# A first mixer's beginning reordered: the condition matvec in four column groups, weight chunks woven between it, late modulation rows moved

## The chip, the cores and the metric

The kernel runs on one core of a Trainium2 chip. The metric is the device time of one execution in microseconds, the median of several. The profile is of one execution; its span is counted from the first to the last instruction. The core has five instruction streams: TensorE (PE, matmuls into PSUM), VectorE (DVE), ScalarE (ACT), GpSimd (POOL) and SyncE (SP, here it issues the DMAs of the weights). They run side by side and wait for each other by semaphores only.

## The reference

Two transformer blocks on 512 tokens of 1024 features, all in fp32. Only the beginning of the first one matters here:

```python
mod_x = (jax.nn.silu(c) @ w_mod[l] + b_mod[l])[:, None, :]
mod_c = jax.nn.silu(c_ctx) @ w_mod[l] + b_mod[l]
sh1, sc1, gt1, sh2, sc2, gt2 = jnp.split(mod_x, N_MOD, axis=-1)
csh1, csc1, cgt1, csh2, csc2, cgt2 = jnp.split(mod_c, N_MOD, axis=-1)
h_x = _modulate(x, g_pre_mix[l], sh1, sc1)       # rmsnorm(x) * (1 + scale) + shift
h_c = _modulate(ctx, g_pre_mix[l], csh1, csc1)
u_x, q_x, k_x, v_x = _project(h_x, w_in[l])      # 1024 x 2048: u, q, k, v of 512 each
u_c, q_c, k_c, v_c = _project(h_c, w_in[l])
attn_x = _neighbourhood_attention(q_x, k_x, v_x, k_c, v_c, rpb[l])
mix_x = jnp.concatenate([_pool_mixer(u_x, pool_w[l], pool_scale[l]), attn_x], axis=-1) @ w_out[l]
```

`w_mod` is 1024 x 6144. Its first two sections (shift and scale, 2048 columns) are needed, for `c` and for `c_ctx`, before any product with `w_in`. The other four are needed for `c` alone, and only later.

## The kernel before

**The stream of weights.** All weights are cut into blocks of 128x128; eight blocks are a chunk of 512 KB. `plan_weights` writes their order down, and SyncE loads the chunks in exactly this order into four buffers `raw`. A chunk is loaded when the user of the chunk four places ahead has let go of its buffer; as SyncE works in order, one late chunk holds up all behind it.

**Splitting.** A product is made of three passes with operands in two parts: a high part rounded to fp32r and the low rest. `ahead` on ScalarE makes the high part `wH` of a chunk (line 1083), `ahead` on GpSimd the low part `wL` (line 2252). There are three buffers of each. The call `ahead(name, k, m)` splits up to three chunks on from the named block, but only such as stand less than four places of the plan behind it (`reach`). The buffer `raw` is free when `wL` is made. Lines 513 to 515 and 550 to 552 are the three passes. The modulation's chunks are not split: those of the first two sections go through TensorE as fp32 matmuls (`first_rows`, line 593), the 32 later ones ("late rows") through VectorE, one multiply-add of 128x1024 each into `macc` (`late_rows`, lines 1667 and 1670). At the end of a section TensorE sums `macc` over the partitions (`late_columns`, line 612).

**The matvec.** The plan begins with 16 chunks `w_mod`, chunk k of a half holding rows 128k of both sections. `first_rows(n)` multiplies the two columns silu(c), silu(c_ctx) with the 1024 columns of the chunk: two matmuls of 512 columns into two banks of two partitions. VectorE copies the two rows out (`first_vectors`, line 1700), `first_columns` (line 602) turns them into columns with eight small matmuls, `first_coefficients` forms shift and scale. The order on TensorE is: chunks 0 to 9, columns of half 0, statistic of x (line 562), chunks 10 to 15. The squares of x are added up by GpSimd (line 2262).

**The norms.** VectorE scales x by the root (line 1732); ScalarE forms `hH` (line 1148), VectorE the full value and every even `hL`, GpSimd every odd `hL` (line 2257). The same is done for ctx: `context_norm` on VectorE (lines 1769, 1775, 1655), `hcH` on ScalarE (line 1181), odd `hcL` on GpSimd.

**The products.** Tiles m=0..3 of `w_in` are u, 4..7 q, 8..11 k, 12..15 v. TensorE works on tiles 0 to 3 as a group (k outside, so that it can start with the first feature block), the statistic of ctx, then tile by tile 4 to 11, tiles 8 to 11 also for ctx and with one pool matmul each (line 659), then the values with tokens as rows (lines 550 to 552). One late row stands in the plan ahead of each of the tiles 4 to 7, two ahead of each of 8 to 11, two behind each value chunk but four more at the end, which VectorE takes up during the attention (one at every eighth step). Behind the values comes the attention: 32 steps of scores (line 569), turn (line 577) and values (line 584), VectorE adding the bias (line 1809), taking the maximum (line 1682) and normalizing (line 1690). The biases `bms` are made by GpSimd (line 2304) from `bra`, which SyncE loads (line 2515).

**One pair of the context norm** stands between two tiles on every engine: ScalarE copies the tile before, then forms two `hcH`; GpSimd splits the tile's chunk, then makes one `hcL`; VectorE does a late row, a pool window and the pair.

## Time and profile before

| | before |
|---|---|
| median of three runs | 1520.77 us (1517.61 to 1526.13) |
| the profiled execution | 1509.5 us, its span 1508.2 us |
| TensorE busy | 1420.2 us, 94% |
| GpSimd / VectorE / ScalarE busy | 48% / 39% / 37% |
| mean granted clock of TensorE | 0.979 |
| first product with `w_in` | 44.06 us |
| last value product, begin of the attention | 182.7 us |
| begin of the product with `w_out` | 281.0 us |

The share of TensorE is an average. A matmul is pipelined, so the duration of one is longer than the distance to the next. In a row of the timeline, the bracket tells how long the engine was idle before the instruction, and which engine's instruction ended that.

### The profile page before, as it was taken

The numbers are of one execution on the slowest core, as the hardware profiler recorded it, in microseconds if no ns is written. First come the engines' busy times: TensorE is split into PE (matmuls) and PEld (weight loads), VectorE is DVE, ScalarE is ACT, GpSimd is POOL, SyncE is SP. The second block draws the span as 40 slices with busy tenths as digits, with TensorE's granted clock in tenths as the row PEclk, the third lists the DMA queues.
The fourth block names the chain that finished last, engine by engine and source line by source line (L and its number), as shares of the span: only waits on it lengthen the run. The fifth ranks groups of instructions, "written<-read, shape, count | busy, mean of one in ns | idle before, by whom it ended". The sixth has DMA issues, their size and how long they took to land.

```text
span 1508.2 us, 16271 instructions
## 1 busy us (share of the span) xinstructions
PE 1420.2 (94%) x6446; PEld 1115.6 (74%) x6446; DVE 589.2 (39%) x872; ACT 551.2 (37%) x865; POOL 717.3 (48%) x387
## 2 busy tenths in 40 slices
PE   8869999988899999999789999999999999999999
PEld 1658766776788887888577778766577788888887
DVE  2592377238342205210362956674444211012110
ACT  3422155354343324422343453653433322122221
POOL 2442343264444443455446957262336655455552
PEclk9989999999999999999899999999999999999999
DMA  8526520323232532333223111111113233233332
GB/s 291 208 103 217 191 81 24 112 82 100 70 112 98 186 115 78 103 98 98 84 56 98 56 43 56 56 57 45 40 43 98 84 98 100 97 97 98 98 98 70
DMA packets 41035, 148.59 MB, mean 99 GB/s; under 512 B 4608, under 2 KB 4864, under 8 KB 40192
## 3 DMA queue, kind: packets, MB, share of 16 engines
q1 hardware_dynamic: 39504, 139.02, 28.7%
q0 software_dynamic: 592, 4.72, 0.9%
q10 hardware_dynamic: 864, 3.82, 0.7%
q8 instruction: 51, 0.84, 0.2%
q14 instruction: 24, 0.20, 0.0%
HBM read 144.65 MB, written 2.10 MB: 97 GB/s over the span
## 4 chain that ended last, share of the span: by engine, by line
PE 73%; DVE 10%; POOL 6%; ACT 5%; issue 4%; DMA 1%; SPq 0%; DVEq 0%; ACTq 0%; POOLq 0%
PE bank L513 20%; PE bank L515 19%; PE bank L514 19%; PE bank L569 3%; POOL wL L2252 3%; PE bank L584 3%; PE bank L562 2%; POOL EE L2399 2%; PE bank L577 1%; DMA raw<-in_wall 1%; PE bank L550 1%; PE bank L552 1%; PE bank L551 1%; DVE xT L1849 1%; ACT wH L1083 1%
## 5 line engine op out<-in xcount | busy, mean ns | idle before, releaser
L2252 POOL TENSOR_TENSOR wL<-raw,wH 128x1024 fp32r<-128x1024 f32 (+1 forms) x205 | 499.4, 2439 | 474.7 <-ACT wH L1083 474.7
L513 PE MATMUL bank<-hH,wH 128*128 128x512 f32 x784 | 320.6, 409 | 41.6 <-POOL wL L2252 26.7
L514 PE MATMUL bank<-hL,wH 128*128 128x512 f32 x784 | 311.1, 397 | 0.0
L515 PE MATMUL bank<-hH,wL 128*128 128x512 f32 x784 | 311.1, 397 | 0.0
L1083 ACT ACTIVATE wH<-raw 128x1024 fp32r<-128x1024 f32 (+1 forms) x205 | 214.6, 1048 | 241.3 <-PE bank L515 168.3
L513 PEld LDWEIGHTS bank<-hH,wH 128*128 128x128 f32 x784 | 151.1, 193 | 82.6 <-issue 43.9
L515 PEld LDWEIGHTS bank<-hH,wL 128*128 128x128 f32 x784 | 150.5, 192 | 33.0
L514 PEld LDWEIGHTS bank<-hL,wH 128*128 128x128 f32 x784 | 151.1, 193 | 30.5 <-issue 1.7
L513 PE MATMUL bank<-gH,wH 128*128 128x512 f32 x352 | 138.2, 393 | 4.1 <-POOL wL L2252 4.1
L514 PE MATMUL bank<-gL,wH 128*128 128x512 f32 x352 | 137.7, 391 | 0.0
L515 PE MATMUL bank<-gH,wL 128*128 128x512 f32 x352 | 137.7, 391 | 0.0
L513 PE MATMUL bank<-bH,wH 128*128 128x512 f32 x256 | 100.4, 392 | 0.0
L515 PE MATMUL bank<-bH,wL 128*128 128x512 f32 x256 | 99.7, 389 | 0.0
L514 PE MATMUL bank<-bL,wH 128*128 128x512 f32 x256 | 99.6, 389 | 0.0
L513 PEld LDWEIGHTS bank<-gH,wH 128*128 128x128 f32 x352 | 66.5, 189 | 19.6 <-issue 5.8
L1113 ACT ACTIVATE P<-bank,small 128x512 f32<-128x512 f32 (+3 forms) x64 | 37.9, 592 | 109.7 <-DVE small L1682 43.0
L515 PEld LDWEIGHTS bank<-gH,wL 128*128 128x128 f32 x352 | 66.5, 189 | 14.0
L514 PEld LDWEIGHTS bank<-gL,wH 128*128 128x128 f32 x352 | 66.4, 189 | 13.9 <-issue 0.2
L2262 POOL TENSOR_TENSOR acc<-acc,tmp 128x512 f32<-128x512 f32 x31 | 41.1, 1326 | 70.6 <-ACT tmp L1107 70.0
L1902 DVE TENSOR_TENSOR tmp<-tmp 128x512 f32<-128x512 f32 x32 | 36.9, 1153 | 90.5 <-ACT tmp L1297 90.5
L1670 DVE SCALAR_TENSOR_TENSOR macc<-raw,vecs,macc 128x1024 f32<-128x1024 f32 x28 | 44.0, 1572 | 38.5 <-DMA raw<-in_wall 37.6
L515 PEld LDWEIGHTS bank<-bH,wL 128*128 128x128 f32 x256 | 48.0, 188 | 10.1
(328 smaller groups left out, 2127.8 us busy)
## 6 DMA issues: line engine op xcount, KB each, us to landing
raw<-in_wall SPq DMA_DIRECT2D x253, 512.0 KB, 3.6
bra<-in_rpbw SPq DMA_DIRECT2D x8, 360.0 KB, 3.3
xq<-in_xt ACTq DMA_DIRECT2D x2, 1024.0 KB, 9.5
xT<-in_xn POOLq DMA_DIRECT2D x1, 2048.0 KB, 8.0
out_x<-xT SPq DMA_DIRECT2D x8, 256.0 KB, 2.0
vE<-in_ctxt ACTq DMA_DIRECT2D x1, 1024.0 KB, 7.9
icn<-in_invc POOLq DMA_DIRECT2D x1, 1024.0 KB, 4.9
xm<-in_memt POOLq DMA_DIRECT2D x1, 1024.0 KB, 6.8
```

The costliest lines, as they stand in the source:

```text
L513: matmul(o, a_h, b_h, start=first, stop=False)
L514: matmul(o, a_h, b_l, start=False, stop=False)
L515: return matmul(o, a_l, b_h, start=False, stop=last)
L562: mm = matmul(o[:, 0:n], ones[lo:hi, :], sq, start=i == 0, stop=i == len(parts) - 1)
L569: mm = matmul(o[:, c0:c1], lhsT, rhs, start=first, stop=last)
L584: mm = matmul(o, v, a.PT[i % 2][:, 128 * n:128 * n + 128], start=n == 0, stop=n == len(values) - 1)
L1083: activation(wH[i % NHL][:, 0:n], raw[c % NRAW][:, 0:n], ACT.Copy).then_inc(s.w_hi, 1)
L1113: activation(a.P[i % 3][:, 0:w], bank[a.sc(i)][:, 0:w], ACT.Exp, bias=small[i % 6][:, 0:1], scale=a.scale, accum_out=small[i % 6][:, 1:2]) ...
L1670: stt(out=macc[:, :], in0=raw[c % NRAW][:, :], scalar=ck, in1=macc[:, :], op0=ALU.mult, op1=ALU.add).then_inc(s.mod_acc, 1)
L1902: tt(t, t, t, ALU.mult).then_inc(s.relu_sq, 1)
L2252: tt(wL[i % NHL][:, 0:n], raw[c % NRAW][:, 0:n], wH[i % NHL][:, 0:n].bitcast(F32), ALU.subtract).then_inc(s.w_lo, 1)
L2262: tt(sums, sums, tm[2 + j % 2][:, :], ALU.add).then_inc(s.add_g, 1)
```

## The change

It moves work within the beginning of the first mixer; the products and sums that are formed are the same.

1. The matvec goes to four column groups. `cond` holds, for each k, silu(c) and silu(c_ctx) in 32 columns, 30 of them zero. The output of matmul i of chunk k goes to the partitions 32(2i + k%2) of bank 6, so that two chunks use four groups; the even and the odd k are summed afterwards. `sel`, a 128x4 matrix of zeros and ones, does that within `first_columns`, which now has four matmuls instead of eight. One copy of 128x512 takes the place of two of 2x512.
2. The plan: 8 matvec chunks, 3 chunks of `w_in` (tiles 0 to 5, k=0..3), 8 matvec chunks, 3 chunks of `w_in` (k=4..7). The first group has six tiles. TensorE takes matvec chunks 8 to 11 behind k=0 and 12 to 15 behind k=1, the second columns behind k=2, the statistic of ctx behind k=7.
3. The squares of x are summed in two halves by GpSimd and VectorE, and the statistic of x is formed between matvec chunks 5 and 6.
4. The pairs of the context norm stand together: all four ahead of tile 6 on VectorE, ScalarE and GpSimd, the splits of tiles 6 and 7 behind them on the latter two, and the copies of u and q behind those.
5. Late rows: none ahead of tile 8, 2, 4, 4 and 6 behind tiles 8 to 11, two behind each value chunk; none is left for the attention. The late columns of sections 2, 3 and 4 stand ahead of tile 11, behind k=1 of the values, and at step 4 of the attention. SyncE's loads of the later biases are moved accordingly.

```diff
@@ -71,16 +71,14 @@
     for half in range(2):
         for k in range(8):
             plan.extend(("w_mod", k, 8 * sec + 4 * half + j, True) for sec in range(2) for j in range(4))
-    group([("w_in", m) for m in range(4)], range(8))
-    for m in range(4, 12):
-        for _ in range(1 if m < 8 else 2):
+        group([("w_in", m) for m in range(6)], range(4 * half, 4 * half + 4))
+    for m in range(6, 12):
+        tile("w_in", m, range(8))
+        for _ in range((0, 0, 2, 4, 4, 6)[m - 6]):
             mod_rows()
-        tile("w_in", m, range(8))
     for k in range(0, 8, 2):
         wide("w_in", 12, range(k, k + 2))
         mod_rows()
-        mod_rows()
-    for _ in range(4):
         mod_rows()
     group([("w_out", m) for m in range(4)], range(8))
     for m in range(4, 8):
@@ -585,22 +586,25 @@
...
         def first_rows(n):
             half, k = divmod(n, 8)
-            pe.wait_ge(raw_in[n % NRAW], 16 * (n // NRAW + 1))
-            pe.wait_ge(s.silu_c, 1)
+            c = ROWS[n]
+            pe.wait_ge(raw_in[c % NRAW], 16 * (c // NRAW + 1))
+            pe.wait_ge(s.silu_c, 2)
+            pe.wait_ge(s.mod_row, half)
             for i in range(2):
-                mm = matmul(bank[2 * half + i][0:2, :], cc[:, 2 * k:2 * k + 2], raw[n % NRAW][:, 512 * i:512 * i + 512],
-                            start=k == 0, stop=k == 7)
+                g = 32 * (2 * i + k % 2)
+                mm = matmul(bank[6][g:g + 32, :], cond[:, k, :], raw[c % NRAW][:, 512 * i:512 * i + 512], start=k < 2,
+                            stop=k >= 6)
             mm.then_inc(s.mod_mm, 1)
         def first_columns(half):
             o = claim(7)
-            pe.wait_ge(s.ident_in, 16)
-            pe.wait_ge(s.mod_row, 2 * half + 2)
-            for j in range(8):
-                mm = matmul(o[:, 2 * j:2 * j + 2], mrow[half][:, 128 * j:128 * j + 128], ident[0:2, 0:2],
-                            start=True, stop=True)
+            pe.wait_ge(s.sel, 3)
+            pe.wait_ge(s.mod_row, half + 1)
+            for j in range(4):
+                mm = matmul(o[:, 4 * j:4 * j + 4], mrow[half][:, 128 * j:128 * j + 128], sel[:, :], start=True, stop=True)
             mm.then_inc(s.mod_col, 1)
             freed[7] = s.mod_ab, 2 * half + 2
@@ -613,16 +617,16 @@
             mm.then_inc(s.mod_sum, 1)
             freed[7] = s.mod_late, sec - 1
-        pe.wait_ge(s.ones, 2)
-        for n in range(10):
+        pe.wait_ge(s.ones, 3)
+        for n in range(6):
             first_rows(n)
-        freed[0:2] = [(s.mod_row, 1), (s.mod_row, 2)]
+        pe.wait_ge(s.add_g, ADD_G.x + 3)
+        pe.wait_ge(s.add_v, ADD_V.x + 3)
+        statistic("x", [(acc[0][:, :], 0, 128), (acc[1][:, :], 0, 128)])
+        first_rows(6)
+        first_rows(7)
         first_columns(0)
-        pe.wait_ge(s.add_g, ADD_G.x + 7)
-        statistic("x", [(acc[0][:, :], 0, 128)])
-        for n in range(10, 16):
-            first_rows(n)
-        freed[2:4] = [(s.mod_row, 3), (s.mod_row, 4)]
+        freed[6] = s.mod_row, 2
         def X1(k):
@@ -631,22 +635,26 @@
         def XC(k):
             return hcH[:, k, :], hcL[:, k, :], s.rest_g if k % 2 else s.rest_v, REST.hc + k // 2 + 1
-        def second_columns(k):
-            if k == 1:
+        def second_half(k):
+            if k < 2:
+                for n in range(8 + 4 * k, 12 + 4 * k):
+                    first_rows(n)
+            if k == 2:
                 first_columns(1)
-        us = [("w_in", m) for m in range(4)]
-        outs = [claim(BANK[t]) for t in us]
-        group(us, range(8), X1, outs, second_columns)
+            if k == 7:
+                pe.wait_ge(s.add_v, ADD_V.c + 7)
+                statistic("ctx", [(acc[1][:, 0:256], 0, 128)], 256)
+        first = [("w_in", m) for m in range(6)]
+        group(first, range(8), X1, [claim(BANK[t]) for t in first], second_half)
         for m in range(4):
             freed[BANK["w_in", m]] = s.u, m + 1
-        pe.wait_ge(s.add_v, ADD_V.c + 7)
-        statistic("ctx", [(acc[1][:, 0:256], 0, 128)], 256)
         for m in range(4, 8):
-            tile("w_in", m, range(8), [(claim(BANK["w_in", m]), X1)])
+            if m >= 6:
+                tile("w_in", m, range(8), [(claim(BANK["w_in", m]), X1)])
             freed[BANK["w_in", m]] = s.q, m - 3
         for m in range(8, 12):
-            if m == 9:
+            if m == 11:
                 late_columns(2)
             b, b2, b3 = BANK["w_in", m], BANK["ctx", m], BANK["pool", m - 8]
             tile("w_in", m, range(8), [(claim(b), X1), (claim(b2)[:, 0:256], XC)])
@@ -1124,41 +1132,52 @@
...
+        ahead("w_in", 0, 0, 1)
         first_norm(0)
-        ahead("w_in", 0, 0)
+        first_norm(1)
+        ahead("w_in", 0, 0, 2)
+        first_norm(2)
+        first_norm(3)
         nc.scalar.dma_start(xc, ctxt).then_inc(s.ctx_in, 16)
         nc.scalar.dma_start(cs[:, O_NA:], cst[:, O_NA:]).then_inc(s.cst_in, 16)
-        first_norm(1)
-        ahead("w_in", 7, 3)
+        ahead("w_in", 0, 0, 3)
+        ahead("w_in", 4, 0, 1)
+        first_norm(4)
+        first_norm(5)
+        ahead("w_in", 4, 0, 2)
+        first_norm(6)
+        first_norm(7)
+        ahead("w_in", 4, 0, 3)
...
@@ -1166,20 +1185,21 @@
...
         root("ctx", 1024, rs[1], 256)
+        for j in range(8):
+            act.wait_ge(s.mult, MULT.hc + j + 1)
+            activation(hcH[:, j, :], tm[j % 2][:, 0:256], ACT.Identity, bias=mod[:, j, 1:2],
+                       scale=coef[:, 1, j:j + 1]).then_inc(s.hi, 1)
+        ahead("w_in", 7, 6, 2)
         act.wait_ge(s.pad, 2)
-        for m in range(4):
+        for m in range(12):
+            if m >= 6:
+                ahead("w_in", 7, m)
             act.wait_ge(s.product, done("w_in", 7, m))
-            activation(up[:, m, 8:520].rearrange("p (r c) -> p c r", c=64),
-                       bank[BANK["w_in", m]].rearrange("p (c r) -> p c r", r=8), ACT.Copy).then_inc(s.u, 1)
-        for m in range(4, 12):
-            ahead("w_in", 7, m)
-            act.wait_ge(s.product, done("w_in", 7, m))
-            if m < 8:
+            if m < 4:
+                activation(up[:, m, 8:520].rearrange("p (r c) -> p c r", c=64),
+                           bank[BANK["w_in", m]].rearrange("p (c r) -> p c r", r=8), ACT.Copy).then_inc(s.u, 1)
+            elif m < 8:
                 copy(qT[:, m - 4, :], bank[BANK["w_in", m]], s.q, 0.125)
-                for j in (2 * m - 8, 2 * m - 7):
-                    act.wait_ge(s.mult, MULT.hc + j + 1)
-                    activation(hcH[:, j, :], tm[j % 2][:, 0:256], ACT.Identity, bias=mod[:, j, 1:2],
-                               scale=coef[:, 1, j:j + 1]).then_inc(s.hi, 1)
             else:
...
@@ -1783,17 +1814,19 @@
             shift(j0 + 1)
         dve.wait_ge(s.rest_g, REST.h1 + 4)
-        for m in range(4, 12):
-            late_rows(1 if m < 8 else 2)
-            if m < 8:
-                window(m - 4)
-                context_norm(2 * m - 8)
-            if m == 9:
-                late_vector(2)
-        for k in range(1, 8, 2):
-            late_rows(2)
-            if k == 3:
-                late_vector(3)
+        for j in range(0, 8, 2):
+            context_norm(j)
+        window(0)
+        window(1)
+        late_rows(2)
+        window(2)
+        late_rows(4)
+        window(3)
+        late_rows(2)
+        late_vector(2)
+        late_rows(8)
+        late_vector(3)
+        late_rows(8)
         dve.wait_ge(s.product, done("w_in", 7, 15))
         nc.vector.tensor_copy(vE[:, 0, :], bank[0]).then_inc(s.v_v, 1)
         nc.vector.tensor_copy(vE[:, 2, :], bank[2]).then_inc(s.v_v, 1)
@@ -2262,35 +2293,40 @@
...
+        ahead("w_in", 0, 0, 1)
         first_norm(1)
+        ahead("w_in", 0, 0, 2)
+        first_norm(3)
+        ahead("w_in", 0, 0, 3)
+        ahead("w_in", 4, 0, 1)
+        first_norm(5)
+        ahead("w_in", 4, 0, 2)
+        first_norm(7)
+        ahead("w_in", 4, 0, 3)
         pool.wait_ge(s.hi, HI.h1 + 8)
         pool.wait_ge(s.full, FULL.h1 + 8)
         nc.gpsimd.dma_start(pw[:, :, :], poolw).then_inc(s.pool_in, 16)
         nc.gpsimd.dma_start(icn[:, :, :], invc.partition_broadcast(128)).then_inc(s.pool_in, 16)
         nc.gpsimd.memset(up[:, :, 0:8], 0.0).then_inc(s.pad, 1)
         nc.gpsimd.memset(up[:, :, 520:528], 0.0).then_inc(s.pad, 1)
-        ahead("w_in", 7, 3)
-        for m in range(4, 12):
+        for j in (1, 3, 5, 7):
+            pool.wait_ge(s.full, FULL.hc + j + 1)
+            rest(hcL[:, j, :], tm[1][:, 0:256], hcH[:, j, :], s.rest_g)
+        ahead("w_in", 7, 6, 2)
+        for m in range(6, 12):
             ahead("w_in", 7, m)
-            if m < 8:
-                j = 2 * m - 7
-                pool.wait_ge(s.full, FULL.hc + j + 1)
-                rest(hcL[:, j, :], tm[1][:, 0:256], hcH[:, j, :], s.rest_g)
...
```

## Rows read from the trace of the kernel before

**Rows 1.** The page: busy time, share of the span, instructions.

```profile
PE 1420.2 (94%) x6446; PEld 1115.6 (74%) x6446; DVE 589.2 (39%) x872; ACT 551.2 (37%) x865; POOL 717.3 (48%) x387
```

**Rows 2.** Table by windows: stretch, its length, busy time of each engine, clock, DMA.

```profile
10.00:20.00 10.00, 9.83 (x23) 1.82 (x22) 0.00 (x0) 3.86 (x7) 8.86 (x7) 1.00 0.98 359
...
100.00:120.00 20.00, 13.63 (x72) 11.69 (x73) 13.66 (x17) 5.32 (x8) 6.68 (x3) 0.83 0.52 184
```

**Rows 3.** Chain of waits: start, length, what.

```profile
2.12 11.91 DMA raw<-in_wall
14.07 12.18 PE bank L593 x28
```

**Rows 4.** Timeline of TensorE: start, length, engine, line; in brackets the idle time before.

```profile
44.06 0.47 PE L513 MATMUL bank<-hH,wH 128*128 128x512 f32 x1 [4.02 <-POOL wL L2252]
...
46.73 0.63 PE L514 MATMUL bank<-hL,wH 128*128 128x512 f32 x1
...
47.15 0.63 PE L515 MATMUL bank<-hH,wL 128*128 128x512 f32 x1
...
69.64 0.59 PE L562 MATMUL bank<-acc,ones 128*128 128x256 f32 x2
...
78.35 0.51 PE L513 MATMUL bank<-hH,wH 128*128 128x512 f32 x1 [2.64 <-POOL wL L2252]
...
117.03 1.84 PE L612 MATMUL bank<-ones,macc 128*128 128x1 f32 x16
...
147.95 0.47 PE L550 MATMUL bank<-wH,hH 128*128 128x512 f32 x1 [0.97 <-ACT up L1094]
```

**Rows 5.** Timeline of VectorE: scaling, rest, window beside a split, one context pair, values.

```profile
31.06 4.91 DVE L1732 TENSOR_TENSOR xq<-xq,rs 128x512 f32<-128x512 f32 x8 [2.40 <-ACT rs L1104]
...
36.53 0.69 DVE L1655 TENSOR_TENSOR hL<-tmp,hH 128x512 fp32r<-128x512 f32 x1
...
81.61 2.78 DVE L1755 TENSOR_TENSOR pa<-pa 128x525 f32<-128x525 f32 x1
...
85.76 0.75 DVE L1769 TENSOR_TENSOR tmp<-vE,rs 128x256 f32<-128x256 f32 x2
...
87.64 0.41 DVE L1775 TENSOR_SCALAR tmp<-tmp,coef,mod 128x256 f32<-128x256 f32 x1
...
182.73 0.69 DVE L1798 COPY vE<-bank 128x512 f32<-128x512 f32 x1 [10.70 <-PE bank L552]
```

**Rows 6.** Transfers of weight chunks in 0 to 60 us, issue to landing.

```profile
DMA to landing us min/median/max: 3.4/4.6/11.9
```

**Rows 7.** Timeline of ScalarE: end of the root of ctx, copies of finished tiles, a split.

```profile
70.77 0.42 ACT L1104 ACTIVATE rs<-rs 128x256 f32<-128x256 f32 x1
...
85.71 0.60 ACT L1094 ACTIVATE qT<-bank 128x512 f32<-128x512 f32 x1 [7.44 <-PE bank L515]
...
127.66 0.60 ACT L1092 ACTIVATE kT<-bank 128x512 f32<-128x512 f32 x1 [6.50 <-PE bank L515]
...
129.10 1.05 ACT L1083 ACTIVATE wH<-raw 128x1024 fp32r<-128x1024 f32 x1
...
136.91 0.60 ACT L1092 ACTIVATE kT<-bank 128x512 f32<-128x512 f32 x1 [6.76 <-PE bank L515]
```

**Rows 8.** Timeline of GpSimd: rest of a context block, a split, the first bias.

```profile
79.31 1.70 POOL L2257 TENSOR_TENSOR hcL<-tmp,hcH 128x256 fp32r<-128x256 f32 x1 [1.01 <-DVE tmp L1775]
...
116.48 2.35 POOL L2252 TENSOR_TENSOR wL<-raw,wH 128x1024 fp32r<-128x1024 f32 x1 [7.19 <-ACT wH L1083]
...
150.80 2.07 POOL L2304 TENSOR_TENSOR bms<-bra,cst 128x256 f32<-128x256 f32 x3 [8.44 <-issue]
```

**Rows 9.** Timeline of SyncE's queue: the first two bias loads.

```profile
147.01 1.92 SPq L2515 DMA_DIRECT2D bra<-in_rpbw  x2
```

**Rows 10.** Timeline of TensorE in the attention, behind a late row.

```profile
220.57 0.66 PE L577 MATMUL bank<-cst,P 128*128 128x128 f32 x4 [0.81 <-DVE P L1690]
```

**Rows 11.** Timeline of VectorE in the attention: the late row.

```profile
215.73 2.30 DVE L1670 SCALAR_TENSOR_TENSOR macc<-raw,vecs,macc 128x1024 f32<-128x1024 f32 x1
```

More of the change, by code:

```diff
@@ L243 @@
 SQ = before(x=8, c=8, xt=8, f=8, h3=8, lat=5, om=4, x2=12)
-ADD_V = before(c=7, m=7, h3=7)
-ADD_G = before(x=7, y=7, f=7, lat=3, om=3, x2=10)
+ADD_V = before(x=3, c=7, m=7, h3=7)
+ADD_G = before(x=3, y=7, f=7, lat=3, om=3, x2=10)
 HI = before(h1=8, hc=8, mix=8, hm=8, h2=8, b=32, h3=8, lat=5, ml=4, h4=8, fb=22)
@@ L389, in build @@
     xq = at("xq", Q, [128, 8, 512])
-    mrow = [at("mrow", Q + (16 + 4 * i) * K, [2, 1024]) for i in range(2)]
+    mrow = [at("mrow", Q + (16 + 2 * i) * K, [128, 512]) for i in range(2)]
+    cond = at("cond", Q + 20 * K, [128, 8, 32])
+    sel = at("sel", Q + 21 * K, [128, 4])
     pa = [at("pa", Q + 2112 * i, [128, 528]) for i in range(2)]
@@ L1161, in scalar_program @@
             if j == 0:
+                act.wait_ge(s.summed, summed("x"))
                 square(acc[1][:, 0:256], xc[:, 0, :], s.sq)
@@ L1693, in vector_program @@
         nc.vector.memset(eps[:, :], EPS).then_inc(s.ones, 1)
+        nc.vector.memset(cond[:, :, :], 0.0).then_inc(s.ones, 1)
+        for j in (3, 5, 7):
+            dve.wait_ge(s.sq, SQ.x + j + 1)
+            dve.wait_ge(s.add_v, ADD_V.x + j // 2 - 1)
+            tt(acc[1][:, :], acc[1][:, :], tm[3][:, :], ALU.add).then_inc(s.add_v, 1)
+        dve.wait_ge(s.ident_in, 16)
+        nc.vector.memset(sel[:, :], 0.0).then_inc(s.sel, 1)
+        dve.wait_ge(s.sel, 1)
+        for i in range(2):
+            g = slice(64 * i, 64 * i + 64)
+            tt(sel[g, 2 * i:2 * i + 2], ident[g, 64 * i:64 * i + 2], ident[g, 64 * i + 32:64 * i + 34],
+               ALU.add).then_inc(s.sel, 1)
         dve.wait_ge(s.vec_in, 16)
@@ L1698, in first_vectors @@
             dve.wait_ge(s.mod_mm, 8 * half + 8)
-            for i in range(2):
-                nc.vector.tensor_copy(mrow[half][:, 512 * i:512 * i + 512],
-                                      bank[2 * half + i][0:2, :]).then_inc(s.mod_row, 1)
+            nc.vector.tensor_copy(mrow[half][:, :], bank[6]).then_inc(s.mod_row, 1)
         def first_coefficients(half):
@@ L1813, in vector_program @@
                 normalize(near, i - 1)
-            if i % 8 == 3 and i < 32:
-                late_rows(1)
-            if i == 28:
+            if i == 5:
                 late_vector(4)
@@ L2262, in add_squares, with first_norm @@
             tt(sums, sums, tm[2 + j % 2][:, :], ALU.add).then_inc(s.add_g, 1)
-        for j in range(1, 8):
-            if j > 1:
-                pool.wait_ge(s.add_g, ADD_G.x + j - 1)
+        for j in (2, 4, 6):
+            if j > 2:
+                pool.wait_ge(s.add_g, ADD_G.x + j // 2 - 1)
             add_squares(acc[0][:, :], j, s.sq, SQ.x)
-        def first_norm(half):
-            for j in range(4 * half + 1, 4 * half + 4, 2):
-                pool.wait_ge(s.full, FULL.h1 + j + 1)
-                pool.wait_ge(s.hi, HI.h1 + j + 1)
-                rest(hL[:, j, :], tm[1][:, :], hH[:, j, :], s.rest_g)
-        first_norm(0)
-        ahead("w_in", 0, 0)
-        first_norm(1)
+        def first_norm(j):
+            pool.wait_ge(s.full, FULL.h1 + j + 1)
+            pool.wait_ge(s.hi, HI.h1 + j + 1)
+            rest(hL[:, j, :], tm[1][:, :], hH[:, j, :], s.rest_g)
+        ahead("w_in", 0, 0, 1)
+        first_norm(1)
+        ahead("w_in", 0, 0, 2)
[6 more added lines that the diff above has]
+        ahead("w_in", 4, 0, 3)
         pool.wait_ge(s.hi, HI.h1 + 8)
@@ L2533, in sync_program @@
                 bias_load(3)
-            if c == late_mod[1] + NRAW:
-                bias_load(4)
-                bias_load(5)
-            if c == late_mod[2] + NRAW:
-                bias_load(6)
-                bias_load(7)
+            if c == first_out + NRAW:
+                for h in range(4, 8):
+                    bias_load(h)
             if c == h_f + NRAW:
```

35 lines of the change are left out of this document (18 added, 17 removed).

## The prediction

> **What bounds the kernel now.** I read the page first: TensorE is busy for 94% of the span [rows 1], so time is won only where it stands still or runs slowly. The table by windows says where that is at the beginning: between 10 and 20 us the DMA queues are full and move 359 GB/s, and between 100 and 120 us TensorE works only 13.63 of 20 us [rows 2]. The chain of waits names the first stretch: a weight chunk that lands after 11.91 us, then the 12.18 us of the condition matvec [rows 3]. The timeline of TensorE gives the stretches after it: the first product starts at 44.06, a wait of 2.64 us follows at 78.35, both for the low part `wL` that GpSimd makes, and the value rows start at 147.95 [rows 4]. The last value product ends at 182.73, when VectorE copies it [rows 5]. That is the mark against which I compare; everything behind the attention that follows it has the same order in both kernels and only shifts.
>
> Two prices recur. At full pace a 512-column product costs 0.229 us: (182.73 - 147.95 - 1.84 for the late columns) / 144 [rows 4, 5]. After a wait they stand 0.42 us apart, still so at 47.15, 3 us after the start at 44.06 [rows 4]: the granted clock is then at 1.2 instead of 2.4 GHz. That is some 9 products, so a restart costs 9 x 0.2, about 1.8 us.
>
> **Part 1, the matvec and the first products.** Before, a chunk costs TensorE four passes of 0.43 us, 1.7 us in all (28 in 12.18) [rows 3]. After, its two matmuls go to different column groups of the array. No row of this trace shows two groups at once, so the bounds are 1.7 us (nothing overlaps) and 0.43 us (two chunks overlap). I take 0.86: two matmuls of one chunk carry no wait between them, the next chunk has one. As the DMA share is 0.98 with 359 GB/s [rows 2], half a megabyte takes 1.46 us to arrive, so at 0.86 the first half is set by transfers. Chunk 3 lands at 14.03 as before, chunk 7 at 14.03 + 4 x 1.46 = 19.9. The statistic of x now stands between chunks 5 and 6 (its two matmuls are four passes, 1.7 us), under the transfers, so half 0 ends near 20.7 instead of 22.9. The squares are summed on two engines by then. Then follow the copy of 128x512 (0.69, as the copy of `vE` [rows 5]), four column matmuls (about 1), coefficients (0.5): 23. Four scalings of x at 4.91/8 us and shift and rest of 1.3 us follow [rows 5]. GpSimd's split of chunk 8 runs from 22 to 24.3, and a VectorE add beside such a split took 2.78 us [rows 5] instead of 0.7, so I charge another 1.5 us. First product at 28.2, 15.9 us earlier than before.
>
> TensorE then does k=0 (18 products, 4.1, and 1.8 for the clock) and chunks 11 and 12 of the second half. Chunks 13 and 14 are new waits: SyncE issues them only when GpSimd has made the low parts of chunks 9 and 10, and GpSimd has a rest of `hL` before each of these. That puts the low parts at 33.3 and 37.8, and a chunk lands no sooner than 3.4 us after its issue [rows 6]. So TensorE waits until about 41.3, and k=1 starts at 42.2 and again slowly: 48.1. Four more chunks (1.7 to 3.4, I take 2), six more k of 4.1 and the columns (1) end the group of six tiles at 75.9. Chunks 19 to 21 are split in good time under it. Before, the same two tiles `m`=4, 5 ended at 85.71 [rows 7]. The lead is 9.8 us; with nothing but TensorE's own work between (28.2 + 8 x 4.1 + 2.7 = 63.7), it would be 22.
>
> **Part 2, the context norm in front of the weight splits.** This is the part that costs. The statistic of ctx follows k=7, and root and statistic took 69.64 to 71.19 before [rows 4, 7], 1.6 us: 77.5. ScalarE and GpSimd now do all eight `hcH` and four `hcL` ahead of chunk 22, and TensorE has nothing but that chunk to go on with. Before, these steps lay between tiles that were ready. One pair of steps took VectorE 85.76 to 88.05, 2.3 us [rows 5]. GpSimd's rest took 1.70 us [rows 8], but beside VectorE's late row; half of a 512-wide rest is 0.65. With one scaling in front of it I take 1.1 and 2.75 for each further pair: 2.3 + 3 x 2.75 + 0.8 = 11.4 us (bounds 10 and 14). The split of chunk 22 takes 2.35 [rows 8]: tile 6 starts at 91.3, 15 us after TensorE ran dry, and slowly (1.8). Tiles 6 and 7 are 24 products of 5.5 us each: 104.1. Tiles 8 and 9 take the 9.25 us that stand between two copies of `kT` [rows 7]. Tile 9's last product ends at 121.7 against 127.6 before [rows 7]: a lead of 5.9, of which 1.8 is only that the late columns now stand in front of tile 11.
>
> **Part 3, chunks that are split too late.** `ahead` splits only chunks whose place in the plan is under the current one plus 4. With two to six rows of modulation between them, chunk 32 (tile 10) is not under 27 + 4, chunk 37 not under 32 + 4, chunk 44 (values) not under 37 + 4. Before, each of these was split one tile early and hidden. Now the split waits until ScalarE has copied the tile before: 1.44 us from the start of `kT` to the split [rows 7], 1.05 for the high part [rows 7], 2.35 for the low part and 0.1 between: 5.0 us after the last product. The pool matmul covers 0.86 of it. So tile 10 waits 4.1 and restarts slowly (1.5): 121.7 + 5.0 + 8.4 + 1.5 = 136.6. The late columns (1.84) hide part of the next one: tile 11 starts at 141.6, waits 2.3, and ends at 151.5 (slow again, 1.5). For chunk 44 GpSimd has the bias ahead of the split: SyncE loads it after the fourth pool matmul, and from that issue at 147.01 to the bias at 150.80 went 3.8 us, the bias itself 2.07 [rows 8, 9]. Before, this lay under the value products, as their first chunk was already split. Now it stands in front: 152.4 + 3.8 + 2.1 + 2.4 = 160.7 for the first value product, against 147.95. Chunk 50 cannot be loaded before late row 17, which follows the late columns of section 3: 1.8 us more wait. Values: 144 x 0.229 + 1.84 + 1.8 + 1.8 = 38.4, end at 199. That is 16.3 us later than 182.73.
>
> **Part 4, the attention without late rows.** A late row took VectorE 2.30 us beside a split, and the wait behind it is 0.81 [rows 10, 11]; such places are two, a third row and the row at the start show less. Gain 1.6 to 4, I take 2.5. The late columns of section 4 only move from step 28 to step 4. Later bias loads stand in front of chunk 60, which is not urgent. Memsets, `sel` and the second Silu (0.3 us) lie under the first transfer.
>
> The sum: 16.3 - 2.5 = 13.8 us more than the span of 1508.2 us; I round to 13.5, about 1522. The profiled execution took 1509.5, 11.3 below the median of 1520.77, all of the shown runs being longer than it; I put the same difference on the median: 1534.
>
> **A rule beside it.** The Trainium skill, "TensorEngine Tiling (Array Packing)", section Theoretical Speedup, states up to 4x where the stationary operand has at most 32 columns. No row here shows it. By it a chunk would cost TensorE 0.43 us; the last four chunks would then be 0.3 us cheaper than I take them and the forecast stays. The same page, section Key Properties, says that a change of tiling mode drains TensorE. That speaks against weaving these chunks between 128-column products; by it each of the four changes costs at most one product, which would add a microsecond.
>
> **The rivals.** (a) The column groups do not overlap. Then a chunk costs 1.7 us, half 0 ends 3.7 later and the four chunks at the end 4.8 later; part of the first is hidden: +7, 1541. For it: no row shows an overlap. Against: nothing in the trace. Chance 0.12. (b) The front and the context norm go better: no blocked VectorE steps (-1.5), chunks 13 and 14 do not hold TensorE back (-5), pairs at 2.4 us (-1): 1526, and down to 1521 with the full 4 us in the attention. For it: the products need only 4.1 us for each k. Against: SyncE's order. Chance 0.14. (c) Faster: the late splits of part 3 cost nothing, because ScalarE and GpSimd have them done before the pool matmul ends. The place is tiles 10, 11 and the first values; the price is 4.1 + 1.5, 2.3 + 1.5, and 8.3 + 1.8, 19.5 us; with it the kernel ends at 1534 - 19.5 - 2 = 1512. It decides from the point where the low part of chunk 32 ends before 122.6. For it: before, no such wait stands at the tiles 9, 10, 11. Against: the condition on the places, which I worked out for each call. Chance 0.07. That the sum holds as it stands, within 7 us: 0.62. The other 0.05 is something unseen, mostly slower.
>
> **How the numbers follow.** Predicted 1534. The range takes (a) and most of (b): 1520 to 1545. About 0.5%, 7.6 us, is what a measurement of this kernel can tell from no change. Faster than that: (c), 0.07. Within: (b) and the lower tail of the main case, 0.23. Slower: 0.70.
>
> **What the changed profile would show.** First product near 28; a wait of some 3 us for a raw chunk near 38; the sixth tile complete near 76; no product for about 15 us behind it while `hcH` and `hcL` alternate; waits of 4, 2 and 8 us in front of tiles 10, 11 and the values, all for `wL`; values complete near 199; attention 2 to 3 us shorter. It would be wrong if tile 6 starts before 85, or if tile 10 follows the pool matmul at once.

## The result, and the profile after

The changed kernel takes 1538.25 us (median of 4 runs, 1533.77 to 1547.15) against 1521.99 us (4 runs) for the kernel before: ratio 1.0114, 95% interval [1.006, 1.0169]. In the second series it is 1544.98 against 1521.66, ratio 1.0160 [1.0131, 1.0189]. The profiled execution took 1538.93 us, span 1537.5.

The page of the changed kernel, busy time by engine:

```profile
PE 1413.9 (92%) x6432; PEld 1118.1 (73%) x6432; DVE 602.8 (39%) x877; ACT 551.0 (36%) x866; POOL 705.1 (46%) x383
```

TensorE has 6 us less to do than in [rows 1], in a span that is 29.3 us longer: time went into standing still. TensorE's waits between 0 and 210 us (line, releaser: us in total, times, longest):

```profile
PE bank L514 <- POOL wL L2283: 20.8, 3, 14.0
PE bank L551 <- POOL wL L2283: 20.3, 2, 17.9
PE bank L598 <- DMA raw<-in_wall: 7.5, 4, 3.6
...
PE bank L514 <- DVE hL L1675: 6.3, 1, 6.3
```

41 us are waits for the low part of a weight chunk, and two of them, 14.0 and 17.9, make most of it. TensorE's timeline shows where, from the matvec to the values (start, length; in brackets the idle time before):

```profile
13.79 4.04 PE L598 MATMUL bank<-raw,cond 128*32 128x512 f32 x12 [0.96 <-DMA raw<-in_wall]
...
29.61 0.79 PE L514 MATMUL bank<-hH,wH 128*128 128x512 f32 x1 [6.32 <-DVE hL L1675]
...
42.81 1.92 PE L598 MATMUL bank<-raw,cond 128*32 128x512 f32 x4 [3.56 <-DMA raw<-in_wall]
50.48 1.92 PE L598 MATMUL bank<-raw,cond 128*32 128x512 f32 x16
...
92.51 0.80 PE L514 MATMUL bank<-hH,wH 128*128 128x512 f32 x1 [13.98 <-POOL wL L2283]
...
127.87 0.77 PE L514 MATMUL bank<-hH,wH 128*128 128x512 f32 x1 [4.23 <-POOL wL L2283]
144.02 0.77 PE L514 MATMUL bank<-hH,wH 128*128 128x512 f32 x1 [2.55 <-POOL wL L2283]
172.68 0.77 PE L551 MATMUL bank<-wH,hH 128*128 128x512 f32 x1 [17.86 <-POOL wL L2283]
195.82 0.50 PE L551 MATMUL bank<-wH,hH 128*128 128x512 f32 x1 [2.40 <-POOL wL L2283]
```

The first product does start 14.5 us earlier than in [rows 4]. It is all given back, and more, in front of tile 6 (13.98) and in front of the values (17.86), which start at 172.68 instead of 147.95. On VectorE the copy that marks the last value product, to be held against the last of [rows 5]:

```profile
212.49 0.69 DVE L1831 COPY vE<-bank 128x512 f32<-128x512 f32 x1 [9.21 <-PE bank L553]
```

The stretches with the waits, by windows (stretch, length, busy time of PE, PEld, DVE, ACT, POOL, clock, DMA share, GB/s):

```profile
80.00:90.00 10.00, 0.00 (x0) 0.00 (x0) 7.02 (x20) 5.83 (x10) 3.08 (x4) 0.60 0.00 1
160.00:180.00 20.00, 7.32 (x22) 5.86 (x23) 1.24 (x1) 2.11 (x2) 6.66 (x5) 0.56 0.44 149
```

In 80 to 90 TensorE does nothing while VectorE and ScalarE make the context norm, and nothing is transferred either: every later chunk waits for buffers that the split behind this norm would free.

### The profile page after: what moved, and what is told of

Read it like the earlier page. It is cut to its first block, busy times and chain, and to the rows that moved or that the text cites. A ratio compares the mean times of both kernels' runs of the same rounds, so it can differ in the third digit from the quotient of the medians.

```text
span 1537.5 us, 16246 instructions
## 1 busy us (share of the span) xinstructions
PE 1413.9 (92%) x6432; PEld 1118.1 (73%) x6432; DVE 602.8 (39%) x877; ACT 551.0 (36%) x866; POOL 705.1 (46%) x383
## 4 chain that ended last, share of the span: by engine, by line
PE 72%; DVE 10%; POOL 6%; ACT 5%; issue 5%; DMA 2%; SPq 0%; DVEq 0%; ACTq 0%; POOLq 0%
PE bank L514 20%; PE bank L515 19%; PE bank L516 19%; PE bank L570 3%; POOL wL L2283 3%; PE bank L585 3%; PE bank L563 2%; POOL EE L2435 2%; DMA raw<-in_wall 2%; PE bank L578 1%; ACT wH L1091 1%; DVE xT L1880 1%; PE bank L551 1%; PE bank L552 1%; PE bank L553 1%
## 5 line engine op out<-in xcount | busy, mean ns | idle before, releaser
L2293 POOL TENSOR_TENSOR acc<-acc,tmp 128x512 f32<-128x512 f32 x27 | 36.1, 1337 | 73.4 <-ACT tmp L1115 73.3
L514 PEld LDWEIGHTS bank<-bH,wH 128*128 128x128 f32 x256 | 48.1, 188 | 10.8 <-issue 1.0
```

Source lines behind the costliest of these rows:

```text
L514: matmul(o, a_h, b_h, start=first, stop=False)
L2293: tt(sums, sums, tm[2 + j % 2][:, :], ALU.add).then_inc(s.add_g, 1)
```

## The experiments

Ratios are to the kernel before in the same series, with their 95% intervals; a ratio under 1 is faster. "The mark" is the copy of the last value product (212.49 above, 182.73 in [rows 5]).

**The changed kernel and the kernel before, once more.** 

> The changed kernel as it is, on the same chip as the three below. Theory (as forecast, plus what its trace showed): 1.011 times the kernel before, some 16 us more; in the trace tile 6 starts near 92, the values start after a wait of over 10 us, near 172. Rival (the 17.9 us in front of the values belong to that one execution): the values start near 161, as forecast, and the span is some 10 us shorter than 1537.5.

1544.98 us, ratio 1.0160 [1.0131, 1.0189]. The wait in front of the values is there again, and so are those at tiles 6, 10 and 11 (13.97, 4.23, 2.55):

```profile
172.44 0.77 PE L551 MATMUL bank<-wH,hH 128*128 128x512 f32 x1 [17.53 <-POOL wL L2283]
```

The mark is at 212.56. So 17.5 is the kernel's own.

> The kernel before, profiled once more. Theory (the profiled execution of before, 1509.5 us, is a quick one of its kind and the forecast's base of 1508.2 is some 10 us under the usual span): this one has a span of 1515 to 1523, the values end within 2 us of 182.7 and the attention or what follows it takes the rest. Rival: the beginning itself varies, the values end near 192.

One execution: 1514.89 us, span 1513.6, first product at 45.44 (44.06 in [rows 4]), the mark at 186.55:

```profile
186.55 0.69 DVE L1798 COPY vE<-bank 128x512 f32<-128x512 f32 x1 [10.82 <-PE bank L552]
```

Neither theory holds wholly: the beginning of the kernel before itself varies by 3.8 us between two executions, and 182.73 was the early one. Between the repeats the mark moves by 26.0 us, between the first two profiles by 29.8.

**At most two late rows between split chunks.** In the plan (cut):

```diff
-        for _ in range((0, 0, 2, 4, 4, 6)[m - 6]):
-            mod_rows()
+        mod_rows()
+        mod_rows()
...
+    for _ in range(4):
+        mod_rows()
```

The last four late rows go back into the attention. The late columns move to where their rows are complete, those of section 2 ahead of tile 10 instead of tile 11. 

> The changed kernel with never more than two late rows between two split chunks: two behind each of the tiles 6 to 11 and of the value chunks, the last four left for the attention as in the kernel before. Theory (part 3 of the forecast): every split is again made one tile early, the waits in front of tile 10, tile 11 and the values go (4.2, 2.5 and 17.9 us and three slow restarts of 1.5), the attention pays 2.4 back: 22 to 28 us less than the changed kernel, so 8 to 12 faster than the kernel before. Rival (the rows are the bound, wherever they stand): the waits come back in front of tile 8 or 9 as waits for late rows and the gain is under 10 us.

1517.93 us, ratio 0.9978 [0.9952, 1.0005]. Tiles 10 and 11 no longer wait, and the values follow the pool matmul:

```profile
93.95 0.80 PE L516 MATMUL bank<-hH,wH 128*128 128x512 f32 x1 [15.39 <-POOL wL L2288]
...
147.39 0.47 PE L553 MATMUL bank<-wH,hH 128*128 128x512 f32 x1 [0.97 <-ACT up L1104]
```

The mark is at 182.17, 30.4 us earlier than in the repeated changed kernel; by the ratios the gain is 0.0182, 27.7 us. So what part 3 is about is worth the whole loss; the forecast had 22.2 us for it (from a lead of 5.9 to 16.3 behind). This run doesn't separate the spacing of the rows from the place of the late columns, which moved too (see part 3 below). The wait at tile 6 stays, at 15.4.

**The splits of tiles 6 and 7 ahead of the context norm.** ScalarE's and GpSimd's programs both get this move (ScalarE's is shown):

```diff
+        ahead("w_in", 7, 6, 2)
         root("ctx", 1024, rs[1], 256)
...
-        ahead("w_in", 7, 6, 2)
```

> The changed kernel with the splits of tiles 6 and 7 ahead of the root and norm of ctx on ScalarE and GpSimd; nothing else is moved. Theory (part 2 of the forecast): TensorE has tile 6 at once behind the statistic of ctx, near 79 instead of 92.5. Tile 7 waits for the copy of u that frees its bank, which still stands behind the norm, near 91. Tile 8 starts near 98.5 instead of 105.2: 6 to 8 us less in all. Rival (the wait of 14 us is owed to the norm itself, which tile 8 needs anyway): tile 8 starts near 105 as before and the time stays.

1538.51 us, ratio 1.0097 [1.0069, 1.0125], 0.0063 or 9.6 us under the repeated changed kernel. The mark moves 7.5 us, to 205.03. Tile 6 has no wait; the one that follows, at tile 7, is shorter:

```profile
89.73 0.79 PE L514 MATMUL bank<-hH,wH 128*128 128x512 f32 x1 [5.85 <-ACT up L1199]
```

Tile 7 now waits for ScalarE to copy `up` out of the bank that it needs. So 7.5 us of the 14 are owed to the order of the split against the norm; the rest stays as the wait for this copy.

**The 2 MB load of x behind the value chunks' low parts.**

```diff
-        nc.gpsimd.dma_start(xT[:, :, :], xn).then_inc(s.xn_in, 16)
...
         for k in range(8):
             ahead("w_in", k, 12)
+        nc.gpsimd.dma_start(xT[:, :, :], xn).then_inc(s.xn_in, 16)
```

> The changed kernel with the 2 MB load of xT issued behind the splits of the first value chunks instead of ahead of the first bias. Theory A: the wait in front of the values grew from the forecast 8.3 us to 17.9 because this load takes the DMA queues just when matvec rows 10 to 15 have to arrive, on which SyncE's bias load hangs. Then six chunks of 1.4 us and the landing remain, the values start near 163 to 165, and the kernel is 7 to 9 us faster than the changed one. Theory B: the late rows, which VectorE takes up only behind the late columns of section 2, are slow by themselves; the start stays near 172 and the time the same within 2 us.

1534.01 us, ratio 1.0077 [1.0061, 1.0092]. The wait falls from 17.53 to 12.02, the mark from 212.56 to 207.13, 5.4 us:

```profile
166.86 0.77 PE L551 MATMUL bank<-wH,hH 128*128 128x512 f32 x1 [12.02 <-POOL wL L2283]
```

The medians fall by 11.0, more than the trace shows in this stretch; the last section has what else differs between executions. Part of what is left of the wait is the order in SyncE's queue. The bias load is issued behind the late rows, of which the last has to leave its buffer first:

```profile
156.10 0.91 SPq L2551 DMA_DIRECT2D bra<-in_rpbw  x2
```

In the changed kernel this is issued at 161.63, in the kernel before at 147.01 [rows 9].

**The first biases behind the low part of the first value chunk.** On GpSimd, in the changed kernel and then in the version with the load moved:

```diff
-        bias(0)
         for k in range(8):
             ahead("w_in", k, 12)
+            if k == 0:
+                bias(0)
```

> The changed kernel with one move on GpSimd: its first work on the attention's biases (three sums, 2.0 us, which wait for a bias load that lands at 168.2 in the changed kernel) comes behind the low part of the first value chunk instead of ahead of it. Theory (the 17.9 us in front of the values are a wait for the bias load, not for the chunk): ScalarE has the chunk's high part at 162.3, so the low part is ready at 164.6 and the first value product runs there, 8 us earlier than 172.7; the biases end at 170.2 and the second chunk's low part at 172.6, ahead of its need at 174.9; values end near 204.6, ratio to the kernel before about 0.005 below the 1.016 of the repeated changed kernel. Rival (the chunk itself is as late, or the second chunk takes the wait over): values still end at 210 or later.

1537.37 us, ratio 1.0102 [1.0045, 1.0159].

```profile
163.21 0.77 PE L551 MATMUL bank<-wH,hH 128*128 128x512 f32 x1 [8.67 <-POOL wL L2283]
```

The wait halves: GpSimd now begins the low part at 160.73 and the biases at 168.20, so the ready chunk had been queued behind the bias. But the chunk was late as well: ScalarE waited 4.26 us for it to land, until 159.52 (5.70 us, until 161.24, in the changed kernel). The mark is at 203.55, about where the theory has it (204.6). The interval of the ratio overlaps that of the repeated changed kernel, so the time alone doesn't show the gain.

> Both: the 2 MB load of x behind the low parts of the value chunks, and the first biases behind the low part of the first one. Theory: the high part of the first value chunk stands at 157.0 (as with the load alone moved), low part at 159.3, first value product there, 7.5 us earlier than the 166.9 of the kernel with the load alone moved; values end near 199.6, the 199 of the forecast; ratio about 1.003. Rival: the second chunk's low part, now behind the biases that start at 162.4, takes the wait over, values end at 204 or later.

1534.85 us, ratio 1.0098 [1.0065, 1.013].

```profile
161.34 0.77 PE L551 MATMUL bank<-wH,hH 128*128 128x512 f32 x1 [5.90 <-POOL wL L2283]
```

Against the version with only the load moved, the mark is 5.1 us earlier (202.08), 2.5 later than expected; 1.8 of that is that the chunk itself landed later (ScalarE's high part starts at 157.66, with only the load moved at 155.90). The time isn't shorter, though: 1.0098 against 1.0077, with overlapping intervals. The attention took 1.5 us more in this profile than in that one; the rest stays open.

**Two column groups of 64 instead of four of 32.** The moving rows are padded to 64 and each matmul of a chunk keeps one group for all k:

```diff
-                g = 32 * (2 * i + k % 2)
-                mm = matmul(bank[6][g:g + 32, :], cond[:, k, :], raw[c % NRAW][:, 512 * i:512 * i + 512], start=k < 2,
-                            stop=k >= 6)
+                g = 64 * i
+                mm = matmul(bank[6][g:g + 64, :], cond[:, k, :], raw[c % NRAW][:, 512 * i:512 * i + 512], start=k == 0,
+                            stop=k == 7)
```

> The changed kernel with the matvec in two column groups of 64 instead of four of 32: the two matmuls of a chunk lie side by side, two chunks do not. Theory: the four chunks that TensorE takes in one go behind k=1 cost 3.4 us instead of 1.9, everywhere else the transfers are the bound: the group of six tiles ends 1.5 us later, the values 1.5 us later. Rival (groups of 64 are not side by side either): 6.9 us for the four, and half 0 ends 3 us later.

One execution, 1549.31 us. Four chunks that have all arrived:

```profile
50.52 3.65 PE L598 MATMUL bank<-raw,cond 128*64 128x512 f32 x16
```

3.65 us against 1.92 with four groups, 0.91 and 0.48 us a chunk: with four groups two chunks overlap as well. Half 0 ends 0.9 us later, the group of six tiles 1.7 (1.5 expected) and the mark 2.9 (215.35). What the last 1.2 are, one execution can't tell.

**The low parts of the first three chunks ahead of the norm's rests on GpSimd.**

```diff
-        ahead("w_in", 0, 0, 1)
-        first_norm(1)
-        ahead("w_in", 0, 0, 2)
-        first_norm(3)
         ahead("w_in", 0, 0, 3)
+        first_norm(1)
+        first_norm(3)
         ahead("w_in", 4, 0, 1)
```

ScalarE's high parts move likewise. 

> The changed kernel with the low parts of the first three split chunks ahead of the two rests of hL on GpSimd (and their high parts earlier on ScalarE). Theory: the wait of 3.6 us for matvec chunk 11 is SyncE's, which issues it only when GpSimd has made the third low part; it goes. VectorE's scalings are blocked beside the three splits, so the first product comes 3 to 5 us later than 29, but k=1 starts near 39 to 41 instead of 44.7 and everything behind it is 4 to 6 us earlier. Rival: the blocked VectorE costs as much as the wait did, the time is the same within 2 us.

1541.27 us, ratio 1.0126 [1.0095, 1.0156]. The wait of 3.56 for the chunk is gone, but the first product comes at 33.80:

```profile
33.80 0.80 PE L514 MATMUL bank<-hH,wH 128*128 128x512 f32 x1 [10.22 <-DVE hL L1674]
```

The splits keep VectorE's scalings and its first rest back by 4 us. Tile 6 comes at 91.11 (92.08 in the repeated changed kernel): 1 us gained, and 1.3 at the mark (211.24), within the 2 us of the rival; the interval of the ratio overlaps both of the changed kernel. The early weight work and the norm pay for each other.

**The two repairs together.** At most two late rows between chunks, the splits ahead of the context norm, the pair copies of `up` woven between the `hcH`, and two late rows ahead of the norm on VectorE. ScalarE's part:

```diff
+        ahead("w_in", 7, 6, 2)
         root("ctx", 1024, rs[1], 256)
...
+            if j % 2:
+                m = j // 2
+                act.wait_ge(s.product, done("w_in", 7, m))
+                activation(up[:, m, 8:520].rearrange("p (r c) -> p c r", c=64),
+                           bank[BANK["w_in", m]].rearrange("p (c r) -> p c r", r=8), ACT.Copy).then_inc(s.u, 1)
+            if j == 5:
+                ahead("w_in", 7, 7)
```

> rows_two and split_first in one kernel, and on top: each copy of u right behind a pair of hcH, the first two late rows ahead of the context norm, the split of tile 8 right behind the norm. Theory: the wait of 14 us in front of tile 6 goes as a whole; tiles 6 and 7 run under the norm, tile 8 starts near 93 instead of 106.5 in rows_two. 12 to 14 us less than rows_two: 0.988 to 0.991 of the kernel before. Rival (transfers of late rows hold tile 8 or 9 back): less than 7 us of that.

1512.38 us, ratio 0.994 [0.9905, 0.9976]: faster than both kernels. The mark is at 174.67, 7.5 us earlier than with the rows alone, where 12 to 14 were expected; the ratio misses the expected 0.988 to 0.991.

```profile
93.12 0.76 PE L516 MATMUL bank<-hH,wH 128*128 128x512 f32 x1 [4.63 <-POOL wL L2292]
107.59 0.47 PE L516 MATMUL bank<-hH,wH 128*128 128x512 f32 x1 [2.86 <-POOL wL L2292]
```

Tile 8 starts where it was expected (93), after a wait of 4.63 us for its low part, which GpSimd makes behind the last `hcL`; so the wait of 14 us is not gone as a whole. Tile 9 waits 2.86 for a chunk whose buffer a late row holds: VectorE takes that row only behind a window, at 96.44.

> The combined version unchanged, once more, on the same chip as the version with the rows moved. Theory: ratio within 0.003 of 0.994, values end at 174.7 plus or minus 1, attention 98 to 103 us long. Rival (its gain was one of the attention's clock): ratio 0.998 or more at the same end of the values.

1511.28 us, ratio 0.9938 [0.9912, 0.9963], the mark at 175.71. The gain holds, though the attention took 104.7 us here where 98 to 103 were expected.

**The third and fourth late row ahead of the first window.**

```diff
+        late_rows(2)
         window(0)
         window(1)
         late_rows(2)
         window(2)
-        late_rows(2)
         window(3)
```

> The combined version, with the third and fourth late row taken by VectorE ahead of the first pooling window instead of behind the second. Theory: the chunk of tile 9 no longer waits for a buffer that a late row holds, tile 9's wait of 2.9 us at 107.6 goes, values start at 137 and end near 171.8, 3 us earlier than 174.7; ratio 0.992. Rival: the windows move back by 2.7 us each, the pooling products and with them the first biases come later, and the wait in front of the values grows from 1.0 to about 4, so that the values end at 174 or later all the same.

1510.03 us, ratio 0.9935 [0.9905, 0.9964]. Tile 9's wait is gone, but tile 8 now waits 5.74 instead of 4.64, and the late columns wait 2.14 for `macc`; the mark is at 175.55, the same. The rival's result, by another way than it named: not the biases but tile 8 and the late columns took the wait over.

## Why the forecast was right, and where it was not

The direction and the places are as forecast; the time, 1538 for 1534, owes part of its closeness to an offset. By its steps:

**Part 1** held in sum. The first product came at 29.61 (28.2). A VectorE step beside GpSimd's split was held up, as charged (1.5): forming the coefficients took 2.29 us and ended with the split. VectorE and GpSimd of the changed kernel, and VectorE of the kernel before, where no split runs beside:

```profile
23.60 2.29 DVE L1742 SCALAR_TENSOR_TENSOR coef<-mod,vecs 128x4 f32<-128x4 f32 x2
```

```profile
23.46 2.34 POOL L2283 TENSOR_TENSOR wL<-raw,wH 128x1024 fp32r<-128x1024 f32 x1 [6.79 <-ACT wH L1091]
```

```profile
28.43 0.24 DVE L1712 SCALAR_TENSOR_TENSOR coef<-mod,vecs 128x4 f32<-128x4 f32 x2
```

The wait for the second half's chunk ended at 42.81 (41.3). The two prices that I took for a chunk were nearly right. One that comes alone fills two of the groups and took 1.05 us, pipelined end included (0.86):

```profile
38.20 1.05 PE L598 MATMUL bank<-raw,cond 128*32 128x512 f32 x4 [1.09 <-DMA raw<-in_wall]
```

Where two have arrived they overlap too: the last four took 1.92 us, 0.48 each, and the sum had 2 for them. The one at 42.81 ran at a granted clock of 0.50 and took the double, 1.92, which the sum had not. Rival (a), no overlap, is dead; the four times of the Trainium skill, "TensorEngine Tiling (Array Packing)", section Theoretical Speedup, is nearly what the rows show: 0.12 us a pass in the row of 1.92, 0.43 in [rows 3]. The drain at a change of mode that the Trainium skill states on the same page, section Key Properties, doesn't show as a gap; the next product starts at 52.33. The group of six tiles ended at 77.9 (75.9), and the root of ctx at 79.5 (77.5), as ScalarE's rows show (the last step, 0.42, starts at 79.07):

```profile
78.57 0.47 ACT L1110 ACTIVATE rs<-bank,eps 128x256 f32<-128x256 f32 x1 [6.90 <-PE bank L563]
```

**Part 2** held: tile 6 at 92.51 (91.3) after 13.98 us (15). The pairs repeat every 2.48 us (I took 2.75). On VectorE and GpSimd, one pair and the split that follows the last:

```profile
82.83 0.42 DVE L1800 TENSOR_TENSOR tmp<-vE,rs 128x256 f32<-128x256 f32 x1 [0.61 <-POOL hcL L2288]
85.32 0.42 DVE L1800 TENSOR_TENSOR tmp<-vE,rs 128x256 f32<-128x256 f32 x1 [0.61 <-POOL hcL L2288]
```

```profile
84.45 0.83 POOL L2288 TENSOR_TENSOR hcL<-tmp,hcH 128x256 fp32r<-128x256 f32 x1 [1.65 <-DVE tmp L1806]
...
90.10 5.17 POOL L2283 TENSOR_TENSOR wL<-raw,wH 128x1024 fp32r<-128x1024 f32 x2
```

VectorE waits for GpSimd to release `tmp`, and GpSimd for VectorE to fill it, in turn. Moving the split ahead took the wait at tile 6 away and gave back 7.5 us, which shows the cause by its removal.

**Part 3** had the right mechanism and one mis-sized term. Tile 10 waited 4.23 (4.1) and tile 11 2.55 (2.3). Rival (c), that late splits cost nothing, was decided at its own point: the low part of chunk 32 only starts at 125.39. But "to the bias 3.8" was read off [rows 8, 9], where the load was issued on time, with fewer transfers beside it (4.4 us to landing there, 6.6 here). In front of the values, which I put at 8.3, stood 17.9. ScalarE and GpSimd of the changed kernel:

```profile
154.85 0.69 ACT L1102 ACTIVATE up<-bank,vecs 128x512 f32<-128x512 f32 x1
161.24 1.06 ACT L1091 ACTIVATE wH<-raw 128x1024 fp32r<-128x1024 f32 x1 [5.70 <-DMA raw<-in_wall]
```

```profile
143.81 0.73 POOL L2330 DMA_DIRECT2D xT<-in_xn  x1
168.20 2.03 POOL L2340 TENSOR_TENSOR bms<-bra,cst 128x256 f32<-128x256 f32 x3 [23.66 <-issue]
170.20 4.66 POOL L2283 TENSOR_TENSOR wL<-raw,wH 128x1024 fp32r<-128x1024 f32 x2
```

and SyncE's queue with the transfers from 136 to 176:

```profile
144.45 17.14 SPq L2586 DMA_DIRECT2D raw<-in_wall  x9
161.63 0.91 SPq L2551 DMA_DIRECT2D bra<-in_rpbw  x2
```

```profile
raw<-in_wall SPq DMA_DIRECT2D x10, 512.0 KB, 5.5
xT<-in_xn POOLq DMA_DIRECT2D x1, 2048.0 KB, 10.4
```

I passed over three things. The six late rows in front of the values are also 3 MB of transfers and nine issues in SyncE's queue ahead of the bias load, which went out at 161.63 and not at the 152.4 that I assumed. And the 2 MB load of x, which I didn't name at all, is issued behind tile 11's split and shares the transfer time with them; in the kernel before it was issued at 141.80, ahead of most of its neighbours, here at 143.81, right ahead of all nine. With the load moved the wait is 12.0, with the biases moved 8.7, with both 5.9: the causes overlap.

The third thing is why nine issues were left at all. Between 129.03 and 144.45 SyncE issued nothing. It waited for a buffer that held the first late row of section 3, and VectorE couldn't take that row before TensorE had summed section 2 (line 616), whose rows VectorE had completed at 121.55. TensorE does that only ahead of tile 11. SyncE's queue, then VectorE:

```profile
127.75 1.28 SPq L2586 DMA_DIRECT2D raw<-in_wall  x3
```

```profile
118.88 2.67 DVE L1690 SCALAR_TENSOR_TENSOR macc<-raw,vecs,macc 128x1024 f32<-128x1024 f32 x2
141.50 0.17 DVE L1696 TENSOR_TENSOR mod<-bank,vecs 128x8 f32<-128x8 f32 x1 [19.95 <-PE bank L616]
```

I had counted this order of rows and columns for chunk 50 and section 3, but not here. Of the 9.6 us too much, 6.8 lie between the end of tile 11's products and the issue of the bias load, and 2.8 between that issue and the biases (6.6 where I took 3.8). The pause of the queue is there with the load moved too (14.5 us) and with the biases moved (15.4). No run moves the late columns of section 2 alone, so what they are worth is not shown; the versions without the long wait put them ahead of tile 10.

From tile 11 (2.4 late) and this wait (9.6) follow the 12.0 that the values start late, and 1.4 in the values themselves (0.6 of it a wait of 2.40 at 195.82 for which I took 1.8) make the mark 13.5 later than 199.

**Part 4** came out in these two profiles: from the mark to the first `w_out` product the attention took 308.39 - 212.49 = 95.9, before 281.00 - 182.73 = 98.3: 2.4 us gained (2.5). But one and the same kernel differs by 6.4 us there (last section), so two profiles don't show it to be the late rows. All 14 speak for it without being a test: the shortest of the eight without late rows in the attention are 95.9 (three of them), the shortest of the six with them 98.3 (two).

**The sum and its offset.** In the span the forecast was +13.8 and the two profiles show +29.3, the repeats +24.0; the medians show +16.3 and +23.3. The +29.3 are 29.8 at the mark, 2.4 less in the attention and 1.9 more behind it. The 13.5 us missing at the mark were covered in the first comparison because I lifted the sum by 11.3, the distance from the profiled execution to the median. For the changed kernel that distance was nothing in the first series (1538.93 against 1538.25) and 6.0 in the second (1539.00 against 1544.98). The profile of before was an early and well-clocked execution, at a mean granted clock of 0.979, where its 13 executions in the second series had 0.967 to 0.976. So the step "the same difference on the median" was an unsupported one that happened to help: it was luck that the time came within 5 us. The range held the time on its slower side, as it would have held the 1544.98 of the repeat only just.

## What to carry to other kernels

When transfers are moved into a stretch, count their bytes and their issues in the queue against everything that is behind them there, also loads that the change doesn't touch; here the first value product came 9.6 us later behind tile 11 than the sum had it. Count also where the queue stands still: a row whose sum another engine has still to fetch holds its buffer, and here no transfer was issued for 15.4 us. A lookahead that is counted in places of a plan (here 4) shrinks when other entries are put between: keep the distance in chunks of work, or count again at each gap. And a serial chain of small steps belongs behind the work that feeds the bottleneck: putting the splits ahead of the norm, the rows two by two and the late columns earlier turned +1.6% into -0.6%.

## What the runs showed of the hardware that I had not expected

Matmuls with 32 stationary columns in four column groups overlap almost completely, from one chunk to the next too: eight fp32 matmuls of 512 columns (16 passes in the trace, 0.43 us each without groups) took 1.92 us, and 3.65 in two groups of 64.

The other was the granted clock at the start of the attention. The combined version was profiled twice. Its windows behind the values, first execution and second:

```profile
175.00:185.00 10.00, 6.55 (x29) 4.91 (x30) 8.54 (x17) 5.53 (x14) 2.82 (x4) 0.91 0.56 152
185.00:195.00 10.00, 10.00 (x57) 7.27 (x55) 7.01 (x14) 4.50 (x11) 1.96 (x2) 0.92 0.28 92
```

```profile
175.00:185.00 10.00, 7.10 (x24) 4.53 (x24) 7.04 (x14) 4.91 (x11) 1.27 (x1) 0.76 0.57 152
185.00:195.00 10.00, 10.00 (x34) 7.01 (x34) 5.60 (x10) 2.53 (x6) 2.22 (x3) 0.50 0.30 92
```

The same instructions run at 0.92 of the clock in one and at 0.50 (1.2 GHz) in the other, 57 matmuls in 10 us or 34, with TensorE busy throughout. From the mark to `w_out` it is 272.94 - 174.67 = 98.3 us in the first and 280.41 - 175.71 = 104.7 in the second. In both, TensorE has worked without a pause from the first value product on (140 to 175 us); then it waits 2 us for the copies, as in all the kernels:

```profile
177.65 0.70 PE L572 MATMUL bank<-kT,qT 64*128 64x256 f32 x2 [1.98 <-DVE vC L1840]
```

With the version that moves the rows the lower level lasts one window longer and the attention 107.8. So behind the same pause of 2 us the same stage took 98.3, 104.7 and 107.8 us, and a profile's time behind such a point tells little about a change ahead of it; marks compared stage by stage do. The times show the two kinds as well: of the seven executions of the combined version in its first series, three took 1502 to 1504 us at a mean granted clock of 0.974 and four 1512 to 1514 at 0.966 or 0.967. What decides it, and whether the pause has a part in it, no run here shows.
